# Hybrid decoder layer on one core: head outputs shifted by DMA and joined on GpSimd, denominators added by VectorE, head loads in column halves

## What is computed

```python
logits = einsum('bqhd,bqkhd->bqhk', q_b, k_sel) * att_scale      # masked
p = softmax(logits)
y_attn = einsum('bqhk,bqkhd->bqhd', p, v_sel)                     # eight heads of 64
y_attn = group_rmsnorm(y_attn, gn_attn, N_HEADS) * silu(az)       # one group a head
y = concatenate([y_conv, y_attn]) @ w_out
out = rmsnorm(x + gate * y, norm_f)
```

## Time and profile before

| | |
|---|---|
| median of the runs | 687.44 us |
| time of the profiled execution | 687.08 us |
| its span, first to last instruction | 685.3 us |
| TensorE busy | 653.4 us (95%) |
| VectorE busy | 452.0 us (66%) |
| ScalarE busy | 376.0 us (55%) |
| GpSimd busy | 240.9 us (35%) |
| DMA moved | 78.64 MB, 115 GB/s in the mean |

### The profile page before, as it was taken

How to read it: one execution, slowest core, us unless ns; L and a number is a source line. 1 busy time by engine, 2 the same in 40 slices (tenths; PEclk the granted TensorE clock), 3 DMA queues, 4 the chain that set the end, 5 groups by cost and what they waited for, 6 DMA issues and landing times.

```text
span 685.3 us, 8984 instructions
## 1 busy us (share of the span) xinstructions
PE 653.4 (95%) x3203; PEld 547.1 (80%) x3203; DVE 452.0 (66%) x750; ACT 376.0 (55%) x547; POOL 240.9 (35%) x133
## 2 busy tenths in 40 slices
PE   0999999999999999999999999999999999999996
PEld 0888987878888888888888888788788887778884
DVE  5884646767889999996038751003899998577625
ACT  6866445655562132444552453444899999874202
POOL 1001234343334152657545856540037635000000
PEclk9999999999999999999999999999999999999998
DMA  8960596443333111111010361134885451222431
GB/s 321 380 229 1 144 170 149 136 155 94 93 92 119 35 50 44 55 38 60 32 63 31 124 215 61 32 89 96 276 193 117 125 124 42 84 92 100 147 123 61
DMA packets 27911, 78.64 MB, mean 115 GB/s; under 512 B 3986, under 2 KB 8410, under 8 KB 27868
## 3 DMA queue, kind: packets, MB, share of 16 engines
q1 hardware_dynamic: 27524, 77.03, 37.5%
q10 hardware_dynamic: 344, 1.05, 0.6%
HBM read 61.25 MB, written 13.41 MB: 109 GB/s over the span
## 4 chain that ended last, share of the span: by engine, by line
PE 82%; DVE 6%; ACT 4%; issue 3%; DMA 2%; POOL 2%; SPq 1%; DVEq 0%; ACTq 0%; POOLq 0%
PE ps L810 17%; PE ps L812 17%; PE ps L811 17%; PE ps L1025 4%; PE ps L1026 4%; PE ps L1027 4%; PE ps L847 3%; PE ps L880 2%; PE ps L881 2%; PE ps L899 2%; PE ps L900 2%; PE ps L968 2%; PE ps L967 2%; PE ps L700 1%; DVE acc L1485 1%
## 5 line engine op out<-in xcount | busy, mean ns | idle before, releaser
L810 PE MATMUL ps<-hH,wH 128*128 128x512 f32 (+1 forms) x544 | 211.7, 389 | 0.1
L812 PE MATMUL ps<-hH,wL 128*128 128x512 f32 (+1 forms) x544 | 210.1, 386 | 0.0
L811 PE MATMUL ps<-hL,wH 128*128 128x512 f32 (+1 forms) x544 | 210.1, 386 | 0.0
L1864 POOL TENSOR_TENSOR wL<-raw,wH 128x1024 fp32r<-128x1024 f32 x35 | 87.7, 2507 | 183.2 <-ACT wH L1083 175.0
L812 PEld LDWEIGHTS ps<-hH,wL 128*128 128x128 f32 x544 | 102.1, 188 | 20.4
L810 PEld LDWEIGHTS ps<-hH,wH 128*128 128x128 f32 x544 | 102.1, 188 | 20.3 <-issue 1.7
L811 PEld LDWEIGHTS ps<-hL,wH 128*128 128x128 f32 x544 | 102.2, 188 | 18.4
L1285 ACT ACTIVATE relu<-ps,wabs 128x384 f32<-128x384 f32 (+5 forms) x48 | 40.1, 849 | 39.5 <-PE ps L900 15.9
L1588 DVE SCALAR_TENSOR_TENSOR score<-relu,wsgn,score 128x384 f32<-128x384 f32 (+5 forms) x42 | 49.7, 1184 | 13.7 <-ACT relu L1285 10.2
L1609 DVE TENSOR_SCALAR_CACHE_REDUCE above<-score,srch 128x384 bf16<-128x384 f32 (+5 forms) x60 | 56.8, 946 | 2.1
L1704 DVE TENSOR_TENSOR phL<-ps,phH 128x512 fp32r<-128x512 f32 (+1 forms) x80 | 49.1, 632 | 10.9 <-ACT phH L1241 10.0
(11 more groups left out here) (240 smaller groups left out, 1170.9 us busy)
## 6 DMA issues: line engine op xcount, KB each, us to landing
raw<-in_w_units SPq DMA_DIRECT2D x36, 512.0 KB, 3.5
ks<-qk_halves SPq DMA_DIRECT2D x32, 256.0 KB, 5.8
xin<-in_x SPq DMA_DIRECT2D x8, 512.0 KB, 7.4
wa<-in_w_ada SPq DMA_DIRECT2D x8, 512.0 KB, 12.1
wa<-in_w_ada SPq DMA_DIRECT2D x16, 256.0 KB, 7.7
gw<-in_w_ada SPq DMA_DIRECT2D x8, 512.0 KB, 4.2
qs<-qk_halves SPq DMA_DIRECT2D x16, 256.0 KB, 4.0
wo<-in_w_out SPq DMA_DIRECT2D x8, 512.0 KB, 7.6
```

Source lines behind the costliest of these rows:

```text
L810: pe.matmul(out, wH[slot(n)][:, kt, :], hH[:, kt, cols], start=(kt == 0), stop=False)
L811: pe.matmul(out, wH[slot(n)][:, kt, :], hL[:, kt, cols], start=False, stop=False)
L812: mm = pe.matmul(out, wL[slot(n)][:, kt, :], hH[:, kt, cols], start=False, stop=(kt == KT - 1))
L1864: g.tensor_tensor(wL[slot(n)][:], raw[slot(n)][:], wH[slot(n)][:].bitcast(F32), ALU.subtract).then_inc(s_wL, 1)
```

## The change

It has five parts.

1. For the outputs g = 0 to 13 (all heads but the last) ScalarE copies the whole 128 rows out of PSUM, into `ya` for even heads and into a new buffer `obuf` for odd ones. SyncE moves the 64 foreign rows to the head's own rows in `tmp` by a DMA inside SBUF (`shift_out`), and GpSimd adds the two (`join`). The PSUM bank counts as read when ScalarE's copy is done (`out_read`). The last head is done as before.
2. VectorE adds the denominators to the group sums out of PSUM (`add_sums`), in place of ScalarE's copy and GpSimd's addition. The square of the second half is no longer split, and its sum is one float32 matmul.
3. The loads of a head are made in column halves (`load_head`): three DMAs for each half, each with 128 destination rows of 2 KB, with one semaphore for each half. The logits of blocks 0 to 3 wait for the first half, those of blocks 4 to 7 for the second.
4. On SyncE the writing of the denominators and their spreading are apart, the w_out tiles come in groups of four and two, and the shifts stand between the loads.
5. The step tables have new values.

```diff
-LOGITS_AT = (1, 3, 10, 13, 14, 15, 16, 18)
-MAX_AT = (1, 2, 9, 14, 14, 15, 15, 18)
-EXP_AT = (9, 13, 13, 16, 16, 17, 19, 21)
+LOGITS_AT = (2, 5, 5, 11, 16, 16, 18, 20)
+MAX_AT = (0, 4, 6, 10, 15, 16, 17, 20)
+EXP_AT = (6, 9, 15, 18, 18, 19, 21, 24)
...
-TMP_AT, OUT_AT = 5, 5
+TMP_AT, OUT_AT = 4, 5
+SHIFTED = 2 * (NH - 1)
...
-SUMS_AT = {HEAD * (2 * t + 2) + 5 + 8 * half: (t, half) for t in range(NT - 1) for half in range(2)}
+SUMS_AT = {HEAD * (2 * t + 2) + 7 + 8 * half: (t, half) for t in range(NT - 1) for half in range(2)}
-KEEP_SUMS_AT = {HEAD * (2 * t + 2) + 5 + 8 * half: (t, half) for t in range(NT - 1) for half in range(2)}
+ADD_SUMS_AT = {HEAD * (2 * t + 2) + 9 + 6 * half: (t, half) for t in range(NT - 1) for half in range(2)}
...
+        def kept_out(g):
+
+            h, sb = g // 2, g % 2
+            return ya[:, h // 2, HALF * sb:HALF * sb + HALF] if h % 2 == 0 else obuf[:]
...
+            def load_head(h, part):
+
+                if h == 2 and part == 0:
+                    sp.wait_ge(s_unit, NU)
+                if h >= 2 and part == 0:
+                    sp.wait_ge(s_lg, NB * (h - 1))
+                if h:
+                    sp.wait_ge(s_stack[part], 48 * h)
+                cols = slice(HALF * part, HALF * part + HALF)
+                sp.dma_start(qs[h % 2][:, cols].bitcast(F32), dqk[0, :, h, :, cols]).then_inc(s_stack[part], 16)
+                for i, dst in enumerate((ks1, ks2)):
+                    sp.dma_start(dst[h % 2][:, cols].bitcast(F32),
+                                 dqk[1, i:i + 1, h, :, cols].broadcast_to([2, HD, HALF])).then_inc(s_stack[part], 16)
+
+            def shift_out(g):
+
+                sp.wait_ge(s_tmp, g + 1)
+                if g:
+                    sp.wait_ge(s_join, g)
+                r, d = rows(g // 2), rows(g // 2 + 1)
+                sp.dma_start(tmp[r, :], kept_out(g)[d, :]).then_inc(s_shift, 16)
+
+            for h in range(2):
+                for part in range(2):
+                    load_head(h, part)
             for h in range(NH):
+                if h:
+                    shift_out(2 * h - 1)
+                if h + 2 < NH:
+                    load_head(h + 2, 0)
+                if h == 0:
+                    load_head(2, 1)
+                if h < NH - 1:
+                    shift_out(2 * h)
+                if h % 2 and h < NH - 1:
+                    keep_row(h // 2)
+                if h == 0:
+                    for ct in range(4):
+                        sp.dma_start(wo[:, ct, :], a["w_out"][P * ct:P * ct + P, :]).then_inc(s_wo, 16)
+                elif h + 2 < NH:
+                    load_head(h + 2, 1)
...
                 if i == 0:
-                    pe.wait_ge(s_stack[h % 2], 96 * (h // 2 + 1))
+                    pe.wait_ge(s_stack[0], 48 * (h + 1))
+                if i == 4:
+                    pe.wait_ge(s_stack[1], 48 * (h + 1))
...
-                if g >= 1:
-                    act.wait_ge(s_o, g)
-                A(tmp[r, :], ps[d, 6 + sb, :], ACT.Copy).then_inc(s_tmp, 1)
+                if g < SHIFTED:
+                    if h % 2 and g > 2:
+                        act.wait_ge(s_join, g if sb else g - 2)
+                    A(kept_out(g), ps[:, 6 + sb, :], ACT.Copy).then_inc(s_tmp, 1)
...
+            def add_sums(t, half):
+
+                dve.wait_ge(s_yss, 2 * t + half + 1)
+                dve.wait_ge(s_ygP, 2 * t + half + 1)
+                dve.wait_ge(s_din, 32 * (t + 1))
+                cols = slice(HALF * half, HALF * half + HALF)
+                v.tensor_tensor(azs[:, t, cols], ps[:, sums_bank(t, half), :], dden[:, cols], ALU.add).then_inc(s_sums, 1)
...
+                g.tensor_tensor(ya[r, h // 2, HALF * sb:HALF * sb + HALF], kept_out(g_)[r, :], tmp[r, :],
+                                ALU.add).then_inc(s_join, 1)
```

More of the change, by code:

```diff
@@ L394, in build @@
         s_wo = sem("s_wo"); s_woH = sem("s_woH"); s_woL = sem("s_woL"); s_woLd = sem("s_woLd")
-        s_stack = [sem(f"s_stack{i}") for i in range(2)]
+        s_stack = [sem(f"s_stack{part}") for part in range(2)]
         s_vh = sem("s_vh"); s_vv = sem("s_vv")
@@ L463, in logit_bank, with out_read @@
             return two((2, 4, 6, 2)[u - 4] if u < NB else 2 - 2 * (u % 2))[:, 0:n]
+        def out_read(engine, g):
+            if g < SHIFTED:
+                engine.wait_ge(s_tmp, g + 1)
+            else:
+                engine.wait_ge(s_o, g - SHIFTED + 1)
+        def kept_out(g):
+            h, sb = g // 2, g % 2
+            return ya[:, h // 2, HALF * sb:HALF * sb + HALF] if h % 2 == 0 else obuf[:]
         def masked_of(u):
@@ L471, in wo_high, with squared @@
             return hH[:, ct, :] if ct < 4 else woB[ct // 2 - 2][:, ct % 2, :]
+        def squared(t, half):
+            return 4 * t + half + (3 if t < NT - 1 else 1)
         def sums_bank(t, half):
@@ L646, in spread_den @@
                                  dd[t, NB * e:NB * e + NB, :].rearrange("(o b) n -> o (b n)", o=1).broadcast_to([HD, S])).then_inc(s_din, 16)
-            for h in range(NH):
-                if h == 2:
[L650 to L653, removed]
-                    for half in range(2):
-                        part = half if i == 0 else i - 1
-                        sp.dma_start(dst[h % 2][HD * half:HD * half + HD, :].bitcast(F32),
-                                     dqk[min(i, 1), part, h, :, :]).then_inc(s_stack[h % 2], 16)
-                if h == 2:
-                    for ct in range(KT - 2):
+            def load_head(h, part):
[10 more added lines that the diff above has]
+                                 dqk[1, i:i + 1, h, :, cols].broadcast_to([2, HD, HALF])).then_inc(s_stack[part], 16)
@@ new lines, in shift_out @@
+            def shift_out(g):
[7 more added lines that the diff above has]
+                    load_head(h, part)
+            for h in range(NH):
+                if h:
[13 more added lines that the diff above has]
+                    load_head(h + 2, 1)
+                if h == 2:
+                    sp.wait_ge(s_wo, 16 * 4)
+                    for ct in range(4, KT - 2):
@@ L1927, in _, with join @@
                     mm.then_inc(s_vv, 1)
-            def pair_square(t, half):
-                pool.wait_ge(s_o, 4 * t + half + 3)
+            def join(g_):
+                h, sb = g_ // 2, g_ % 2
+                r = rows(h)
+                pool.wait_ge(s_shift, 16 * (g_ + 1))
+                if g_ % 4 == 3:
+                    pool.wait_ge(s_ygP, g_ // 2)
+                elif g_ % 4 == 2:
+                    pool.wait_ge(s_join, g_)
+                elif g_ % 4 == 0 and g_:
+                    pool.wait_ge(s_ygP, g_ // 2)
+                elif g_ == 1:
+                    pool.wait_ge(s_join, 1)
+                elif g_ % 4 == 1:
+                    pool.wait_ge(s_woL, g_ // 4 + 1)
+                g.tensor_tensor(ya[r, h // 2, HALF * sb:HALF * sb + HALF], kept_out(g_)[r, :], tmp[r, :],
+                                ALU.add).then_inc(s_join, 1)
+            def pair_square(t, half):
+                if t < NT - 1:
+                    pool.wait_ge(s_join, 4 * t + half + 3)
+                else:
+                    pool.wait_ge(s_join, 4 * t + half + 1)
+                    pool.wait_ge(s_o, half + 1)
                 if t or half:
@@ L1972, in _ @@
                     out_split(1)
+            join(SHIFTED - 1)
             pair_square(NT - 1, 0)
```

90 lines of the change are left out of this document (48 added, 42 removed).

## The result

The changed kernel takes **852.0 us** (median; 851.6 to 853.7 over 5 runs) against 687.15 us (686.0 to 687.8) for the kernel before on the same chip: ratio **1.2412 [1.2398, 1.2426]**. The forecast was 849 us with the range 818 to 915. The span of the profiled execution is 849.8 us, where 847.1 was predicted.

The account below looks back on a forecast made before the run. Head loads on two DMA engines were taken as the bound: 455.2 + 1.3 + 262 (loads) + 15 (other transfers) = 733.5 us, plus 113.6 to the end = 847.1 us span, 849 us measured time; range 818 to 915 us.

Parts of the forecast that it names:

- The number of engines: Head loads in the attention stage: source outermost extent 2 confines each load to the same two DMA engines, formerly 16.
- One load: A 256 KB head load on two engines at 24 GB/s each takes 5.46 us (4.97 to 6.04).
- rival (c): Head loads: two engines at only 15.4 GB/s each, 8.5 us a load, 1003 us in all; chance 0.03.
- The other transfers and dry stretches: Until head 7's last load, w_out tiles, denominator spreads and shifts add 15 us on the two engines, which never run dry.
- my sixteenths: Every other 16-engine DMA puts a sixteenth of its bytes on each of the two load engines: 15 us in sum.
- The group sums only in heads with 20 us to spare: Attention stage: group sums wait for late joins only in heads with 20 us to spare, so at no cost.
- up to 16 us late: Shifts also pass the two load engines, so each lands behind the load queued ahead, up to 16 us late.
- The way to the end: From head 7's fifth logits block to the end: 113.6 us, with its later step and a lower clock cancelling.
- the bounds: The forecast's own limits: 823 us with 4.97 us a load, 879 with 6.04, up to 892 with the lower clock.
- rival (a): Loads spread over 16 engines stay hidden; lighter VectorE and ScalarE gain 1.5 us, giving 686 us; chance 0.09.
- The bound of 4.2 us: Attention stage: the most lighter VectorE and ScalarE can give back, if all seven heads were as short as the shortest.
- the last exponential just before its transposes: New step tables: this placement costs a few tenths of a us a head at full speed, 2 us in rival (a).

Follow-up runs that it names:

- experiment 1: The changed kernel with each head's loads as 12 DMAs of 64 plain rows (128 KB each), all else kept: 686.89 us, ratio 1.0009 to the kernel before.
- the doses: The kernel of experiment 1 with each load's 64 rows taken at outermost extent 2, 4, 8 or 16: 852.56, 733.59, 694.93, 686.00 us.
- experiment 7: The kernel of experiment 1 with the last block's exponential two steps earlier: 689.27 us; in a second kernel, with nearly the old step tables instead: 697.65 us.
- experiment 4: A separate kernel that only copies x and times loads by outermost extent, row count and queue; queued 256 KB loads of extent 2 finish 5.13 us apart.

## Why the prediction was right, and where its terms were not

- **The number of engines** (two, by completion writes) was right: 2 a load in the changed kernel, 16 in experiment 1, and the times of the doses follow it.
- **One load**: 5.46 us predicted, 5.13 measured. An engine moves 131,072 bytes in 5.13 us, 25.6 GB/s, near the upper end of the bounds taken from the earlier trace rows; rival (c), 15.4 GB/s from the earlier trace rows, is out. 48 loads are 246 us and not 262.
- **The other transfers and dry stretches**: 15 us were given. The last head load lands at 730.0 us, where 733.5 was forecast. From 456.4 us that is 273.6 us, so some 27 us were not head loads, 12 more than my sixteenths of the others' bytes. The pair was not dry: the DMA digits of 455.5 to 700 us never fall under 1, and by its packets the trace has two or more under way in all but 1.7 of the 273.6 us. The sixteenths were right too: where two w_out tiles and a shift lie between two loads, these land 8.0 us apart, 5.13 + 2.9. Most of the 12 us stands elsewhere. In five places, from 540, 579, 614, 650 and 717 us, two loads take 11.6 to 12.6 us together in place of 10.3, 9.4 us in sum, though nothing else lands on the pair there; each time the other 14 engines are carrying their shares of w_out tiles or of spread denominators. So the pair runs slower beside busy neighbours; why it does is not shown. The two errors, -16 and +12, nearly cancel.

```profile
DMA  1111111111111185212123121162121151121121
```

- **"The group sums only in heads with 20 us to spare"** was wrong. They held TensorE for 36.1 us in three goes. The reason is in the step before: I had put the shifts "up to 16 us late" and then let them lie in time that was free. SyncE's timeline, and the issues in the DMA view of 720 to 734 us (count, KB, us to landing), show the last such chain:

```profile
719.96 0.54 SPq L689 DMA_DIRECT2D tmp<-obuf  x1
```

```profile
tmp<-obuf SPq DMA_DIRECT2D x1, 128.0 KB, 11.6
```

  Issued at 719.96, landed 11.6 us after, join 1.3 and square 1.0 us: the group sum's matmul at 734.10, and behind it the fifth logits block at 736.68. Most of the three holds costs nothing in the end, since the loads flow on meanwhile; only the last one moves the end. Without it the block could have started at 730.0, when its operands were in, 6.7 us sooner: an estimate, from the landing and from TensorE's idle time before it.
- **The way to the end**: 113.6 us forecast from the fifth logits block of head 7, 849.8 - 736.68 = 113.1 measured. I had let the clock cancel against the later place of the block, and it does to 0.5 us. Windows (columns as in the earlier trace rows) show the clock low behind the 12 us of waiting and at full speed from 739 us on: 5 us at 0.63 are 5 x 0.37 = 1.9 us of work lost, and the first 2.6 of these 5 us belong to the group sum and the transposes ahead of the block.

```profile
667.00:672.00 5.00, 4.97 (x13) 3.44 (x14) 1.94 (x4) 1.30 (x3) 1.27 (x1) 0.50 0.13 51
...
721.00:734.00 13.00, 0.77 (x5) 0.34 (x3) 2.58 (x6) 1.31 (x4) 2.26 (x2) 0.62 0.21 54
734.00:739.00 5.00, 4.90 (x16) 3.44 (x17) 2.12 (x5) 1.35 (x4) 4.63 (x5) 0.63 0.13 30
739.00:760.00 21.00, 19.53 (x107) 15.67 (x106) 12.84 (x23) 18.59 (x29) 3.69 (x3) 1.00 0.32 107
```

- **Together**: span 849.8 against 847.1. The mechanism was right, but that the two lie only 2.7 us apart is luck in part: the loads took 16 us less, the rest on the pair 12 more, the group sum held the block for 6.7, and the way behind it was 0.5 shorter. In the bounds one sum leaves out the 1.3 us from issue to first bytes: with 4.97 us a load it gives 824.5 us and not 823; the range doesn't hang on it.
- **What the other edits are worth** (rival (a), 686 us): experiment 1 gives 686.9. Of the 1.5 us forecast as a gain nothing is measured. The bound of 4.2 us for lighter VectorE and ScalarE was read from the shortest head of the earlier trace rows and left TensorE out: its idle time did fall by 2.2 us in 106 (experiment 1), and the heads came no faster. And the last exponential just before its transposes was priced as a cost of a few tenths of a us a head; experiment 7 shows the other sign, 2.4 us lost when it comes two steps earlier.
- **The Trainium skill's rule** in "DMA: Bandwidth & Descriptors", section "Rules for kernel authors", on an outermost dim below 16, now has counts for 2, 4, 8 and 16 from this case, and they agree. The other page that I drew on, "SBUF — State Buffer" of the Trainium skill, section "Door 1: The DMA port swizzle", says that partitions 0 to 63 reach only 8 of 16 ports. That is not what sets these loads apart: in experiment 4 four loads to 64 rows of 4 KB moved 202 GB/s over their whole stretch (104.9 to 110.1 us) and four to 128 plain rows of 2 KB 223 (93.95 to 98.65 us), which is far from twice, and far from the 350 and more that I expected. What held the loads of before at 246 GB/s stays open.

## What to carry to other kernels

Count the completion writes of a DMA before its bytes: packets under 512 B divided by the number of DMAs is how many of the 16 engines carry it, and it is set by the outermost extent that remains after joining. A repeated or split source that saves DMAs on paper can cost four fifths of their bandwidth (51 GB/s here against 246 in the earlier trace rows); a layout in which the pieces stand next to each other, or more DMAs of plain rows, costs nothing measurable. When one transfer becomes the bound, each small DMA on the same engines becomes a wait of its own; another queue made that wait shorter here (some 5 us in place of 13 to 14) but not free.

## What of the hardware was not expected

- SyncE's issue of a load is blocked, 5.00 us each, once three such loads are under way. Nothing but the length of the issue instruction shows it.
- One engine's rate is 25.6 GB/s in rows of 2 KB, with the other 14 idle; four queued loads of the same size on 16 engines move 223 GB/s over their whole stretch (extent 16 at 80.5 to 85.2 us of experiment 4), 14 each.
- Beside busy neighbours the pair is slower: 11.6 to 12.6 us for two loads in place of 10.3, in five places of the changed kernel.
- TensorE's granted clock fell to 0.73 in the mean over 510 to 530 us, in which it was busy for 7.6 of 20 us, where the earlier trace rows has 1.00 at 19.8. Of the two levels, 1.2 and 2.4 GHz, that is a mix; the 5 us from 667 us, right behind the 12.32 us in which TensorE waited for the second group sum, ran wholly at the lower one (0.50). Over the whole execution the mean was 0.906.
